# Picks behind the transposes with 17 more rows, and seven batches of first one-hots on GpSimd

## What is computed

```python
q = (x @ w_query)                        # 8 heads x 2 halves of 128
s = q . sub_keys                         # scores against 128 keys a half
s1, i1 = top_k(s[:, :, 0], 16); s2, i2 = top_k(s[:, :, 1], 16)
top_s, pos = top_k(s1[..., None] + s2[..., None, :], 16)
idx = i1 * 128 + i2 at pos               # 128 experts of 16384 for a token
gates = softmax(top_s)
act = gelu(expert_u[idx] . x)
out = h + sum(gates * act * expert_v[idx])
```

## Time and profile before

| | us |
|---|---|
| runs | 2550.41, 2552.13, 2559.08; median 2552.13 |
| the profiled execution | 2544.61 |
| its span in the trace | 2542.9 |
| TensorE busy | 2468.2 (97%) |
| VectorE busy | 1975.3 (78%) |
| GpSimd busy | 1438.6 (57%) |
| ScalarE busy | 424.2 (17%) |

### The profile page before, as it was taken

The page is one execution under the profiler, slowest core; times in us unless marked ns, Lnnn a source line. Parts: engine busy times, 40 slices in busy tenths (PEclk is TensorE's granted clock), DMA queues, the critical chain, the costliest instruction groups (busy, mean ns, idle before and its releaser), DMA issues.

```text
span 2542.9 us, 24120 instructions
## 1 busy us (share of the span) xinstructions
PE 2468.2 (97%) x7561; PEld 1356.1 (53%) x7561; DVE 1975.3 (78%) x4252; ACT 424.2 (17%) x782; POOL 1438.6 (57%) x1169
## 2 busy tenths in 40 slices
PE   8999999999889999999999999999999999999998
PEld 7687886868665344444444444444444444444443
DVE  4308799768888878778798877879888787888886
ACT  0213313224984000200010000000000000000001
POOL 0000276687401467577576766767676776767673
PEclk9999999999999999999999999999999999999999
DMA  8544776864868799999999999999999999999995
GB/s 333 217 158 165 307 247 191 325 164 86 264 181 277 282 379 389 386 353 406 397 372 420 420 393 399 381 411 419 420 420 402 402 402 413 417 418 419 419 420 219
DMA packets 288079, 857.68 MB, mean 337 GB/s; under 512 B 42064, under 2 KB 99408, under 8 KB 273360
## 3 DMA queue, kind: packets, MB, share of 16 engines
q0 software_dynamic: 167184, 541.73, 55.5%
q1 hardware_dynamic: 108416, 289.25, 30.1%
q10 hardware_dynamic: 12352, 25.17, 2.6%
HBM read 807.75 MB, written 48.30 MB: 337 GB/s over the span
## 4 chain that ended last, share of the span: by engine, by line
PE 61%; DMA 15%; POOL 13%; issue 6%; ACT 3%; DVE 1%; SPq 1%; ACTq 0%; DVEq 0%
PE pairs L831 19%; PE pairs L785 17%; PE pairs L699 15%; POOL ring L679 13%; DMA ring<-in_expert_u,idx 7%; DMA ring<-in_expert_v,idx 6%; PE pairs L742 4%; PE pairs L717 2%; ACT arena L985 2%; PE pairs L769 1%; PE pairs L798 1%; ACT arena L1009 1%; DMA arena<-gate_tables 1%; DVE arena L1197 1%; ACT arena L987 0%
## 5 line engine op out<-in xcount | busy, mean ns | idle before, releaser
L679 POOL DMA_INDIRECT ring<-in_expert_u,idx x512 | 644.7, 1259 | 626.2 <-DVE dots L1186 355.5
L831 PE MATMUL pairs<-arena 128*128 128x512 f32 x2048 | 888.7, 595 | 15.0 <-DVE arena L1252 13.2
L785 PE MATMUL pairs<-arena 128*128 128x512 f32 x2048 | 882.5, 592 | 0.0
L1186 DVE CUSTOM_DVE_ANT_0 junk<-ring,xf 128x1024 bf16<-128x1024 f32 x512 | 612.0, 1223 | 163.4 <-DMA ring<-in_expert_u,idx 159.9
L679 POOL DMA_INDIRECT ring<-in_expert_v,idx x512 | 581.2, 1135 | 265.9 <-issue 119.9
L831 PEld LDWEIGHTS pairs<-arena 128*128 128x128 f32 x2048 | 390.5, 191 | 510.8 <-issue 507.9
L785 PEld LDWEIGHTS pairs<-arena 128*128 128x128 f32 x2048 | 388.6, 190 | 486.5 <-issue 486.5
L1197 DVE SCALAR_TENSOR_TENSOR arena<-ring,arena 128x1024 f32<-128x1024 f32 x381 | 475.6, 1284 | 96.0 <-DMA ring<-in_expert_v,idx 94.8
L699 PE MATMUL pairs<-arena 128*128 128x256 f32 (+1 forms) x1792 | 393.2, 382 | 5.9 <-ACT arena L946 4.7
L699 PEld LDWEIGHTS pairs<-arena 128*128 128x128 f32 x1792 | 341.2, 191 | 55.9 <-ACT arena L946 5.4
L993 ACT ACTIVATE arena<-pairs 128x512 f32<-128x512 f32 x128 | 76.1, 597 | 1068.0 <-PE pairs L785 1042.2
(11 more groups left out here) (174 smaller groups left out, 1059.2 us busy)
## 6 DMA issues: line engine op xcount, KB each, us to landing
arena<-in_w_all SPq DMA_DIRECT2D x80, 1024.0 KB, 6.6
arena<-in_uT SPq DMA_DIRECT2D x128, 512.0 KB, 6.7
arena<-in_expert_v SPq DMA_DIRECT2D x128, 512.0 KB, 9.0
arena<-gate_tables SPq DMA_DIRECT2D x32, 1024.0 KB, 10.0
gate_tables<-arena SPq DMA_DIRECT2D x11, 2048.0 KB, 9.1
gate_tables<-junk ACTq DMA_DIRECT2D x4, 2048.0 KB, 13.8
ring<-in_expert_u,idx POOLq DMA_INDIRECT x512, 9.0
ring<-in_expert_v,idx POOLq DMA_INDIRECT x512, 9.6
```

The costliest lines, as they stand in the source:

```text
L679: nc.gpsimd.indirect_dma_start(out=ring[:, r % RING, :], out_offset=None, in_=expert_u if table == "u" else expert_v, in_offset=bass.Indir ...
L785: last = nc.tensor.matmul(score_bank[x], uslot[:, x % USLOTS, k * P:(k + 1) * P], xfT[:, k, :], start=(k == 0), stop=(k == KD - 1))
L831: last = nc.tensor.matmul(o_bank[n % 4], gated[:, x % GSLOTS, t * P:(t + 1) * P], vrows[:, j, half * 512:(half + 1) * 512], start=(j == 0) ...
L1186: nc.vector.tensor_tensor_reduce(out=junk[:, r % 2, :], in0=row, in1=xf[:, t % 2, :], scale=1.0, scalar=0.0, op0=ALU.mult, op1=ALU.add, ac ...
```

## The change

1. `FILL`: in groups 1 and 2 "outp" gets 0 us and "query" 82 and 84 us instead of 66. The pick of ranks 0 and 2 so moves to the head of the "query" list, and the list has rows 0 to 26 in group 1 (before, 0 to 18) and 27 to 56 in group 2 (before, 19 to 39): 64 rows ahead of the table stage instead of 47.
2. In `order`, a pick (and its keep) stands at least 8 rows behind its digits.
3. `BY_POOL`, batches 11, 17, 23, 29, 35, 41 and 47, get their first one-hots from GpSimd, eight `tensor_scalar` instructions each, placed in its list ahead of row `rows + RING` (72). ScalarE makes those of the other 17 odd batches.

```diff
-        for gate, y, y2, outp, query in ((0.0, 0.0, 0.0, 0.0, 0.0), (4.0, 13.0, 6.0, 2.0, 66.0), (4.0, 13.0, 6.0, 2.0, 66.0), (0.0, 8.0, 0.0, 0.0, 66.0))]
+        for gate, y, y2, outp, query in ((0.0, 0.0, 0.0, 0.0, 0.0), (4.0, 13.0, 6.0, 0.0, 82.0), (4.0, 13.0, 6.0, 0.0, 84.0), (0.0, 8.0, 0.0, 0.0, 66.0))]
...
-        PLACES_US = 10.0
+        PLACES_US, PLACES_ROWS = 10.0, 8
...
             if unit[0] == "pick" and held:
                 order.append(held.pop())
+                rows_since = 0
+            rows_since += unit[0] == "row"
             if unit[0] == "digits":
                 held.append(unit)
+            elif unit[0] == "pick" and rows_since < PLACES_ROWS or unit[0] == "keep" and pick_late:
+                pick_late.append(unit)
             else:
                 order.append(unit)
+            if rows_since >= PLACES_ROWS:
+                order += pick_late
+                pick_late = []
...
+        BY_POOL = [b for b in range(BATCHES) if b % 6 == 5 and b > 5]
+        BY_ACT = [b for b in range(BATCHES) if b % 2 == 1 and b not in BY_POOL]
...
+            def first_hots(b):
+                c = b % HOTBUFS
+                pool.wait_ge(table_full, 2 * (b - HOTBUFS) + 2)
+                if b // (P // HOTS) > 0:
+                    pool.wait_ge(turned_out, b // (P // HOTS))
+                for t in range(HOTS):
+                    k = b * HOTS + t
+                    last = nc.gpsimd.tensor_scalar(hots[:, c, 0, t, :], iota[:], routeT[:, 0, k:k + 1], None, ALU.is_equal)
+                last.then_inc(hot_pool, 1)
...
+                    if r == rows + RING:
+
+                        for b in BY_POOL:
+                            first_hots(b)
...
-                if b % 2 == 1:
-                    pe.wait_ge(hot_first, b // 2 + 1)
+                if b in BY_ACT:
+                    pe.wait_ge(hot_act, BY_ACT.index(b) + 1)
+                elif b in BY_POOL:
+                    pe.wait_ge(hot_pool, BY_POOL.index(b) + 1)
...
-                if b % 2 == 1 and b + 2 < BATCHES:
+                if b % 2 == 1 and b + 2 in BY_ACT:
                     first_hots(b + 2)
```

7 lines of the change are left out of this document (5 added, 2 removed).

## The result

The changed kernel takes 2570.43 us (median of 5 runs, 2569.56 to 2573.84), the kernel before beside it 2550.79 (5 runs, 2546.96 to 2559.08). The ratio is 1.0069, 95% interval 1.0052 to 1.0086: the change is slower by 0.7%, as forecast (2568). (The ratio is taken over the runs and is not the quotient of the two medians, 1.0077.) The profiled execution has a span of 2568.3 us, against 2542.9.

The account below looks back on a forecast made before the run. TensorE bounds the kernel nearly throughout, with VectorE as tight before the table stage and ScalarE busiest in it. Terms 20.4 + 11.4 - 8 - 8 = +15.8 us on the median 2552.1 gave 2568, own range 2557 to 2580.

Parts of the forecast that it names:

- Part 1: Picks of ranks 0 and 2 moved behind norm_h: cost 0, covered by VectorE's 10.58 us wait for ScalarE's places.
- Part 2: Eight more rows ending group 1's query part: late landings make TensorE lose 20.4 us, lower bound 5.5.
- the wait named: TensorE's wait of some 17 us at the sum of squares in group 2, which needs VectorE's sums.
- rival 1: Rows 19 to 26 and group 2's as fast as VectorE: cost 5.5 + 7, whole 2549 us; chance 0.18.
- Part 3: Nine more rows in group 2's query part: 8.8 us wait plus 2.6 slow clock, 11.4 us (7 to 19).
- TensorE loses 24.1 - 3.7: Group 1's rows: VectorE 24.1 us late, less 3.7 slack up to the output projection, gives 20.4 us.
- Part 4: Table stage: seven batches' first one-hots on GpSimd relieve ScalarE, -8 us (9.6 less 1.6 for late arrival).
- the speed: Table stage: GpSimd's one-hots take 0.29 us each, 3.4 us a batch; from about 0.7 us each TensorE is held up.
- arrival: Table stage: GpSimd reaches batch 11 at 34 us, ready at 37.5, 2.2 us late for TensorE; 1.6 taken off.
- Part 5: Dense stage with 17 rows less: TensorE's waits shrink, -8 us (bounds 0 and 10.7).
- Rival 2: Table stage: GpSimd's one-hots hold VectorE up 16 us, whole 2584 us; chance 0.13.
- the mark set for it: Table stage: VectorE's L1467 lasting more than 0.34 us beside GpSimd's new instructions would show the forecast wrong.

Follow-up runs that it names:

- e6: Changed kernel without the 17 more rows and without GpSimd's one-hots, only the picks moved; 2553.03 us, ratio 0.9989 to the kernel before.
- e4: Changed kernel without GpSimd's one-hots, SyncE's load of the next hT behind three more weight loads; 2561.41 us, ratio 1.0036 to the kernel before.
- e5: Kernel before, with the first one-hots of batches 11, 19, 27, 35 and 43 on GpSimd; 2550.41 us, ratio 0.9984.
- e2: Changed kernel without GpSimd's one-hots (picks and 17 rows alone); 2569.38 us, ratio 1.0072 to the kernel before.
- e3: Kernel before with 15 instead of 8 rows ahead of the second pick, 62 ahead of the table stage; 2548.23 us, ratio 0.9984.
- e11: Changed kernel without GpSimd's one-hots and without group 1's eight more rows, 56 rows in all; 2555.41 us, ratio 0.9994 to the kernel before.
- e8: e3 with the load order of e4 and the five GpSimd batches of e5; 2544.02 us, ratio 0.9956 to the kernel before.

## Why the prediction was right, point by point

- **Part 1, the picks, 0**: right, as far as e6 can tell (ratio 0.9989, the interval reaches over 1). The wait for the places takes them: it is 5.20 us instead of 10.58.
- **Part 2, rows 19 to 26, 20.4**: right in size and in mechanism. Row 26 was used by 357.0 (forecast 356.0), TensorE lost 21.0 us, 17.01 of them in the wait named. That the landings of the very rows were taken (17.3 us is the median of the last two), and not VectorE's 1.15 us, decided it; rival 1 would have had 5.5. The burst is shown as a cause by e4, for 8 of the 21 us.
- **Part 3, rows of group 2, 11.4**: its two terms, 8.8 for the wait and 2.6 for the slow clock, measured 8.1 and 3.0. What the sum did not have is 3.8 us of small waits between the sum of squares of group 2 and group 3. The step that failed is "TensorE loses 24.1 - 3.7": it let VectorE's lateness end with one wait. VectorE reached its next deadlines late as well, and each cost a little.
- **Part 4, the one-hots, -8**: the term that was mis-sized; measured -1.2 in the stage, and +1.8 in the hand-over takes it back. The step is the speed. I took 0.29 us an instruction from AFFINE_SELECT as the nearest row and 3.4 us a batch; the rows show a median of 0.604 us and 5.5 to 6.4 us a batch. The point from which it would matter was put at 0.7 us an instruction, and eight in 5.6 us are just that. (No instruction ran alone: each of the 56 has VectorE's one-hots beside it, and in each batch one is beside L1495 and takes 1.45 to 1.85 us.) The other half of the term, what a batch off ScalarE's list gives, was right: in e5 eight batches take 24.3 us instead of 26.45, 2.1 less, forecast 1.9. But the forecast let every one of the seven batches fit. At 5.5 to 6.4 us the place decides: TensorE waits 2.24 us for a batch that is the fourth behind a score tile (17 and 41), 3.21, 1.38 and 1.09 for the sixth or eighth (11, 35, 29), nothing for the second (23 and 47). TensorE's idle time in the stage did fall, from 159.1 - 132.2 = 26.9 to 157.9 - 135.9 = 22.0 us, by 4.9 instead of 8; but its busy time rose by 3.7, since the clock went to 0.50 behind two of the new waits:

```profile
710.00:712.00 2.00, 2.00 (x10) 0.50 1.15 348
733.00:735.00 2.00, 2.00 (x11) 0.50 1.02 291
810.00:812.00 2.00, 2.00 (x20) 1.00 1.01 291
```

- The other condition of part 4, **arrival**, was off too, to the good: GpSimd came 703.45 - 673.0 = 30.4 us into the stage, as before, not at 34. The stage had moved back as far as GpSimd's list had, so the 4 us between them, worked out from TensorE's slack, weren't there.
- **Part 5, the dense stage, -8**: measured -12.0. All waits behind the first tile went, 8.1 us, and TensorE's busy time fell by 3.9, 1692.8 to 1688.9, the slow clock behind them; I had left some of the waits in for rows spread anew. The four kernels with 56 to 64 rows ahead and no one-hots moved (e2, e3, e4, e11) take 1687.4 to 1688.9 us and have under 1 us of waits there, so this is the floor. The hand-over's wait grew from 6.23 to 8.10 us instead of shrinking.
- **The sum**: 31.8 - 8 - 8 = +15.8 forecast; 36.5 - 1.2 + 1.8 - 12.0 = +25.1 by the profiles, +19.6 by the medians. The errors (+4.7 before the stage, +6.8 in it, -4.0 in the dense stage, +1.8 at the hand-over) partly cancel by the profiles; of the 9.3 us that are left the medians show 3.8, since the profiled execution of the kernel before was a fast one. That the median came within 3 us of the forecast is in part luck.
- **Rival 2** (GpSimd's one-hots hold VectorE up by their whole length, 16 us) is false in its size. It is not nothing: the mark set for it, L1467 over 0.34 us beside them, is met. VectorE's own one-operand one-hots as groups (count, busy us, mean ns), before, in e2 and in the changed kernel:

```profile
L1467 DVE TENSOR_SCALAR arena<-iota,arena 128x128 f32<-128x128 f32 x384 | 101.3, 344 | 25.5 <-PE pairs L798 25.5
```
```profile
L1499 DVE TENSOR_SCALAR arena<-iota,arena 128x128 f32<-128x128 f32 x384 | 101.5, 364 | 25.5 <-PE pairs L830 25.5
```
```profile
L1499 DVE TENSOR_SCALAR arena<-iota,arena 128x128 f32<-128x128 f32 x384 | 105.7, 356 | 18.4 <-PE pairs L830 18.4
```

The seven kernels without one-hots on GpSimd have 101.2 to 101.5 us here, the seven with them 105.0 to 105.7 (neighbours overlap, so the busy time tells more than the mean). Single ones of the changed kernel in the view of line L1499, at 704 to 705.8 us beside GpSimd's batch 11 and at 720 to 721.9 us with GpSimd idle (shortest, median and longest in ns):

```profile
L1499 DVE TENSOR_SCALAR arena<-iota,arena x7: 331/375/466, 703.7 to 705.6; 128x128 f32<-128x128 f32 x7
```
```profile
L1499 DVE TENSOR_SCALAR arena<-iota,arena x8: 335/336/338, 720.0 to 721.8; 128x128 f32<-128x128 f32 x8
```

So both run at once and VectorE is slowed a little, by 4 us in all and not by 16. Beside VectorE's two-input one-hot it is GpSimd that yields: its fourth instruction of batch 11 starts at 705.60 and lasts 1.84 us, beside L1495 (705.84, 1.21 us, as always); its neighbours take 0.59 to 0.85.

```profile
705.60 1.84 POOL L683 TENSOR_SCALAR arena<-iota,arena 128x128 f32<-128x128 f32 x1
707.43 0.59 POOL L683 TENSOR_SCALAR arena<-iota,arena 128x128 f32<-128x128 f32 x1
```

The Trainium skill (SBUF — State Buffer, "Who interferes with whom") says that a VectorE instruction with two inputs in SBUF contends with a GpSimd instruction that reads SBUF; the trace agrees, 1.84 against 0.59 us. Of the rule of the 2-port modes, on which rival 2 stood, the full exclusion isn't seen: `tensor_scalar` ran on both engines at once, 0.60 us on GpSimd and 0.375 instead of 0.336 on VectorE. Whether VectorE was in such a mode, no run shows.

## What to carry to other kernels

Work that is moved into an engine's tight stretch costs what its data take to land, not what the engine takes for it: put it into a wait that the profile shows (with 15 rows ahead of the pick in the 10 us wait, 62 rows ahead cost 9 us of start; 64 rows, with the extra ones at the stretch's end, 34). A helper engine helps only at the item for which the next engine really waits, and an engine's speed for a new instruction should be taken from that instruction, with the point from which it matters worked out first. A gain in front of a stage that another engine bounds can come back as that engine's waits (all of e5's 7.3 us did, 4.4 of e8's 5.6), so the two have to be changed together. And a profile to compare with should be a typical execution: the one of the kernel before lay 6 us under its median.
